# Part of a 31-tap depthwise convolution moved to ScalarE and GpSimd, and 64x64 matrix products spread over four quadrants of TensorE

## The reference, cut to what matters

```python
def causal_dwconv(x, w, b):
    K, C = w.shape                       # K = 31, C = 1024
    y = lax.conv_general_dilated(
        x, w[:, None, :], window_strides=(1,), padding=[(K - 1, 0)],
        dimension_numbers=("NWC", "WIO", "NWC"), feature_group_count=C)
    return y + b

def conformer_conv(x, norm, w1, b1, dw_w, dw_b, ln_g, ln_b, w2, b2):
    h = rms_norm(x, norm) @ w1 + b1
    h = jax.nn.glu(h, axis=-1)
    h = causal_dwconv(h, dw_w, dw_b)
    h = jax.nn.silu(layer_norm(h, ln_g, ln_b))
    return h @ w2 + b2
```

```python
def rwkv_step(S, inp):
    r_t, w_t, k_t, v_t, kk_t, a_t = inp
    sa = jnp.einsum('dbhij,dbhj->dbhi', S, -kk_t)
    S = (S * w_t[..., None, :] + sa[..., :, None] * (kk_t * a_t)[..., None, :]
         + v_t[..., :, None] * k_t[..., None, :])
    y = jnp.einsum('dbhij,dbhj->dbhi', S, r_t)
    return S, y
```

## Time and profile before

| | before |
|---|---|
| median of three runs | 2742.05 us |
| the profiled execution: device time, span | 2743.26 us, 2742.0 us |
| mean granted TensorE clock | 0.965 |
| busy over the span: PE, DVE, ACT, POOL | 93%, 55%, 36%, 8% |
| conformer tile loop, from the glu of tile 0 to the sum of tile 7 | 814.5 to 969.8 us |
| the four quarters of the mixers | about 1850 to 2265 us |

### The profile page before, as it was taken

One profiled execution on the slowest core, in us unless ns is written; L12 is line 12 of the kernel. 1 busy time (PEld: TensorE's weight loads), 2 busy tenths in 40 slices (PEclk: granted clock), 3 DMA queues, 4 the chain that ended last, 5 costly groups with the idle time before them and its releaser, 6 DMA issues. The chain is left out here.

```text
span 2742.0 us, 42005 instructions
## 1 busy us (share of the span) xinstructions
PE 2560.1 (93%) x17980; PEld 1960.5 (72%) x17980; DVE 1499.9 (55%) x1996; ACT 1000.1 (36%) x1467; POOL 220.8 (8%) x190
## 2 busy tenths in 40 slices
PE   8989999999999999999999999997888787979997
PEld 6767878888878877778888878776677675733332
DVE  6776455454559875455454565735675746431112
ACT  4454333232346653243232343325353433321111
POOL 1002010000010000010000110001101100123331
PEclk9999999999999999999999999997998898989998
DMA  4223223222221122222222235322111133389994
GB/s 172 83 73 129 95 77 106 95 92 95 106 93 47 62 92 85 74 104 94 98 101 92 92 142 181 133 92 70 23 31 24 20 79 134 113 351 386 382 380 187
DMA packets 94280, 334.77 MB, mean 122 GB/s; under 512 B 39312, under 2 KB 44688, under 8 KB 60304
## 3 DMA queue, kind: packets, MB, share of 16 engines
q1 hardware_dynamic: 80272, 323.66, 33.1%
q0 software_dynamic: 13824, 8.44, 1.0%
HBM read 368.20 MB, written 30.93 MB: 146 GB/s over the span
## 5 line engine op out<-in xcount | busy, mean ns | idle before, releaser
L557 PE MATMUL bank<-xg_hi,w_hi 128*128 128x512 f32 x1504 | 597.7, 397 | 12.1 <-DVE xg_lo L579 12.1
L557 PE MATMUL bank<-xg_hi,w_lo 128*128 128x512 f32 x1504 | 586.6, 390 | 0.0
L557 PE MATMUL bank<-xg_lo,w_hi 128*128 128x512 f32 x1504 | 586.5, 390 | 0.0
L544 DVE TENSOR_TENSOR w_lo<-w_raw,w_hi 128x2048 fp32r<-128x2048 f32 x165 | 378.7, 2296 | 194.2 <-ACT w_hi L540 194.1
L540 ACT ACTIVATE w_hi<-w_raw 128x2048 fp32r<-128x2048 f32 x165 | 314.3, 1906 | 229.4 <-PE bank L557 206.3
L557 PEld LDWEIGHTS bank<-xg_hi,w_hi 128*128 128x128 f32 x1504 | 282.8, 188 | 77.5 <-DVE w_lo L544 12.0
L557 PEld LDWEIGHTS bank<-xg_lo,w_hi 128*128 128x128 f32 x1504 | 282.9, 188 | 63.8 <-issue 6.0
L557 PEld LDWEIGHTS bank<-xg_hi,w_lo 128*128 128x128 f32 x1504 | 282.6, 188 | 59.2
L557 PE MATMUL bank<-f_h_hi,w_hi 128*128 128x512 f32 x384 | 151.5, 394 | 0.0
L557 PE MATMUL bank<-f_h_hi,w_lo 128*128 128x512 f32 x384 | 150.6, 392 | 0.0
L557 PE MATMUL bank<-f_h_lo,w_hi 128*128 128x512 f32 x384 | 149.2, 389 | 0.0
(11 more groups left out here) (492 smaller groups left out, 4523.8 us busy)
## 6 DMA issues: line engine op xcount, KB each, us to landing
w_raw<-stream SPq DMA_DIRECT2D x165, 1024.0 KB, 4.8
e_over_ring<-expert_rows SPq DMA_DIRECT2D x70, 1024.0 KB, 9.9
e_w_raw<-expert_rows SPq DMA_DIRECT2D x26, 1024.0 KB, 8.3
p_spill<-p_stage SPq DMA_DIRECT2D x36, 256.0 KB, 2.2
na_bias<-bias_na SPq DMA_DIRECT2D x32, 160.0 KB, 4.9
mix_gate<-p_spill SPq DMA_DIRECT2D x16, 256.0 KB, 2.8
e_w_raw<-y_rows SPq DMA_DIRECT2D x8, 512.0 KB, 6.6
rw_rkv<-p_spill SPq DMA_DIRECT2D x12, 256.0 KB, 4.9
```

What stands on the lines that cost most here:

```text
L544: V.tensor_tensor(ring(m)["lo"][m % SLOTS][:, :], ring(m)["raw"][m % RAW][:, :], ring(m)["hi"][m % SLOTS][:, :].bitcast(F32), ALU.subtract ...
L557: return T.matmul(out_ap, lhsT, rhs, start=first, stop=last, skip_group_check=True)
```

## The change

Two things are changed.

1. **Convolution.** TensorE keeps taps 0 to 7 (CONV_C_PE = 8), VectorE keeps taps 18 to 29, ScalarE keeps tap 30. Taps 8 to 17 (CONV_C_POOL = 10) are multiplied by ScalarE: an activation with the tap as scale, the first straight into a sum (c_mu or c_inv, which are free in this stage), nine into three rotating buffers (two halves of `square`, and `root`). GpSimd (`pool_conformer`) adds the nine to the sum, one after the other; a product waits until the addition three before it has been made. VectorE adds the bank and then GpSimd's sum to c_h (`sums(j)`), after tap 22 of the next tile, and for the last tile at the end. ScalarE's diagonals of taps 4 to 7 (in its order) are written in the next turn of the loop.
2. **Mixers.** `products` takes its two banks together and goes over i, then q, then e, so all four quadrants take turns. A product AB, and a new one BL (B times A once more), write the other half ("crossed"), so that X and LT lie in swapped halves; ScalarE copies LT from BL, and VectorE makes XT0 from BA. U reads the half 1-e and writes e. X (read e, write 1-e) and XT (read e, write e) of a level are interleaved. MN goes over four corners, and Z over q within i.

```diff
 LEVELS = 6
-CONV_C_PE = 13
...
+    c_pool = list(range(CONV_C_PE, CONV_C_PE + CONV_C_POOL))[::-1]
+    c_pool_base = CONV_C - 1 - c_pool[0]
+    c_pool_sum = [c_mu, c_inv]
+    c_product = [square[:, 0, :], square[:, 1, :], root[:, :]]
+
+    def c_product_at(j, m):
+        return (j * (CONV_C_POOL - 1) + m - 1) % 3
     c_last_tap = CONV_C - 2
...
+    def pool_conformer(G):
+        for j in range(KT):
+            total = c_pool_sum[j % 2]
+            for m in range(1, CONV_C_POOL):
+                s = CONV_C - 1 - c_pool[m]
+                G.wait_ge(*act_c.at("product", j, m))
+                if m > 1:
+                    G.wait_ge(*pool_c.now())
+                G.tensor_tensor(total[:, s:], total[:, s:], c_product[c_product_at(j, m)][:, s:], ALU.add).then_inc(
+                    *pool_c.mark("tap", j * (CONV_C_POOL - 1) + m - 1))
...
+        def diags(j, first, last):
+            for m in range(first, last):
+                k, n = c_order[m], j * CONV_C_PE + m
+                if n >= 4:
+                    A.wait_ge(*pe_c.at("conv", n - 4))
+                A.activation(c_diag_hi[:, n % 4, :], const("ident"), ACT.Copy, scale=c_tap(j)(k)).then_inc(
+                    *act_c.mark("diag_hi", n))
+                A.wait_ge(*dve_c.at("taps_lo"))
+                A.activation(c_diag_lo[:, n % 4, :], const("ident"), ACT.Copy,
+                             scale=c_taps_lo[:, CONV_C * j + k:CONV_C * j + k + 1]).then_inc(*act_c.mark("diag", n))
+
+        def products(j, first, last):
+            for m in range(first, last):
+                k, at = c_pool[m], c_product_at(j, m)
+                s = CONV_C - 1 - k
+                n = j * (CONV_C_POOL - 1) + m - 1
+                if n >= 3:
+                    A.wait_ge(*pool_c.at("tap", n - 3))
+                A.activation(c_product[at][:, s:], c_t1[:, j % 2, 0:S - s], ACT.Copy, scale=c_tap(j)(k)).then_inc(
+                    *act_c.mark("product", j, m))
+
         for j in range(KT):
...
             A.activation(c_h[:, j, :], c_t1[:, i, :], ACT.Identity, scale=c_tap(j)(CONV_C - 1),
                          bias=vcol("c_dw_b", j)).then_inc(*act_c.mark("last_tap", j))
+            if j:
+                diags(j - 1, 6, CONV_C_PE)
             if j >= 2:
-                A.wait_ge(*pe_c.at("conv", n_diag - len(c_order) - 1))
+                A.wait_ge(*pe_c.at("conv", (j - 1) * CONV_C_PE - 1))
             A.activation(c_t_hi[:, i, C_PAD:], c_t1[:, i, :], ACT.Copy).then_inc(*act_c.mark("t_hi", j))
+            if j >= 2:
+                A.wait_ge(*dve_c.at("h", j - 2))
+            A.activation(c_pool_sum[i][:, c_pool_base:], c_t1[:, i, 0:S - c_pool_base], ACT.Copy,
+                         scale=c_tap(j)(c_pool[0])).then_inc(*act_c.mark("product", j, 0))
+            products(j, 1, 4)
             if j + 1 < KT:
                 act_take(A, place[("pw1", j + 1)])
...
+            for m in range(4):
+                diags(j, m, m + 1)
+                products(j, 4 + m, 5 + m)
+            products(j, 8, CONV_C_POOL)
+        diags(KT - 1, 4, CONV_C_PE)
...
+        def sums(j):
+            V.wait_ge(*pe_c.at("conv", (j + 1) * CONV_C_PE - 1))
+            V.wait_ge(*dve_c.now())
+            V.tensor_tensor(c_h[:, j, c_base:], held("conv", j)[:, c_base:], c_h[:, j, c_base:], ALU.add).then_inc(
+                *dve_c.mark("conv", j))
+            V.wait_ge(*pool_c.at("tap", (j + 1) * (CONV_C_POOL - 1) - 1))
+            V.wait_ge(*dve_c.now())
+            V.tensor_tensor(c_h[:, j, c_pool_base:], c_pool_sum[j % 2][:, c_pool_base:], c_h[:, j, c_pool_base:],
+                            ALU.add).then_inc(*dve_c.mark("h", j))
 
         pointwise(0)
...
-            for k in range(CONV_C_PE, CONV_C - 1):
+            first = CONV_C_PE + CONV_C_POOL
+            for k in range(first, CONV_C - 1):
                 s = CONV_C - 1 - k
                 V.wait_ge(*dve_c.now())
                 stt(V, c_h[:, j, s:], c_t1[:, i, 0:S - s], c_tap(j)(k), c_h[:, j, s:], ALU.mult, ALU.add).then_inc(
                     *dve_c.mark("tap", j, k))
-                if k == CONV_C_PE:
+                if k == first + 4 and j:
+                    sums(j - 1)
+                if k == first + 1:
                     V.wait_ge(*act_c.at("t_hi", j))
                     V.tensor_tensor(c_t_lo[:, i, C_PAD:], c_t1[:, i, :], c_t_hi[:, i, C_PAD:].bitcast(F32),
                                     ALU.subtract).then_inc(*dve_c.mark("t_lo", j))
             if j + 1 < KT:
                 pointwise(j + 1)
-            n_last += len(c_order)
-            V.wait_ge(*pe_c.at("conv", n_last))
-            V.wait_ge(*dve_c.now())
-            V.tensor_tensor(c_h[:, j, c_base:], held("conv", j)[:, c_base:], c_h[:, j, c_base:], ALU.add).then_inc(
-                *dve_c.mark("h", j))
+        sums(KT - 1)
         dve_keys(V, 1, 0, 1)
...
+            def products(name, lhs, rhs, freed_by, freed, cross=0):
+                b = [take_bank(T, (name, t, d, q), freed_by, freed, t, q) for q in range(2)]
+                for i in range(4):
+                    for q in range(2):
                         for e in range(2):
                             rows, c = half_rows(q ^ e), half_rows(2 * i + e)
-                            mm = matmul(T, b[half_rows(e), i * HEAD:(i + 1) * HEAD], lhs[rows, c], rhs[rows, c])
-                    mm.then_inc(*done.mark(name, t, q))
...
+            def block_product(b, n, e, out_half, lhs, rhs):
+                return matmul(T, b[half_rows(out_half), n * HEAD:(n + 1) * HEAD], lhs[half_rows(e), n, :],
+                              rhs[half_rows(e), n, :])
 
             T.wait_ge(*by_dve.at("B", t))
-            products("AB", A_, B, by_dve, "X0")
-            products("BA", B, A_, by_act, "LT")
+            products("AB", A_, B, by_dve, "X0", 1)
+            products("BL", B, A_, by_act, "LT", 1)
+            products("BA", B, A_, by_dve, "XT0")
             yield
...
-                block_products(b, one["LT"], one["X"]).then_inc(*done.mark("U", t, l))
+                for n in range(8):
+                    for e in range(2):
+                        mm = block_product(b, n, 1 - e, e, one["LT"], one["X"])
+                mm.then_inc(*done.mark("U", t, l))
...
                 T.wait_ge(*by_act.at("U", t, l))
                 if l < LEVELS - 1:
-                    b = take_bank(T, ("X", t, d, l), by_dve, "X", t, l)
-                    block_products(b, XT, one["U"]).then_inc(*done.mark("X", t, l))
+                    b_x = take_bank(T, ("X", t, d, l), by_dve, "X", t, l)
                 b = take_bank(T, ("XT", t, d, l), by_dve, "XT", t, l)
-                block_products(b, one["U"], XT).then_inc(*done.mark("XT", t, l))
+                for n in range(8):
+                    for e in range(2):
+                        if l < LEVELS - 1:
+                            mx = block_product(b_x, n, e, 1 - e, XT, one["U"])
+                        mm = block_product(b, n, e, e, one["U"], XT)
+                if l < LEVELS - 1:
+                    mx.then_inc(*done.mark("X", t, l))
+                mm.then_inc(*done.mark("XT", t, l))
                 yield
             T.wait_ge(*by_dve.at("XT", t, LEVELS - 1))
...
+            corners = [(par, e, half_rows(par), half_rows(e)) for par in range(2) for e in range(2)]
+            for i in range(4):
+                o, o2 = slice(i * HEAD, (i + 1) * HEAD), slice((4 + i) * HEAD, (5 + i) * HEAD)
+                for par, e, hc, rows in corners:
+                    matmul(T, b_eo[e][hc, o], UW[rows, par, i, HEAD:P], tokB[rows, i, hc])
+                for par, e, hc, rows in corners:
+                    matmul(T, b_eo[e][hc, o2], tokB[rows, i, hc], UW[rows, par, i, 0:HEAD], True, False)
+                for par, e, hc, rows in corners:
+                    mm = matmul(T, b_eo[e][hc, o2], tokK[rows, i, hc], rw_tokV[rows, i, hc], False, True)
...
-                A.wait_ge(*by_dve.at("XT0", t, q))
-                A.activation(one["LT"][:, fours(q), :], blocks(held("BA", t, d, q), 4), ACT.Copy).then_inc(
+                A.wait_ge(*by_pe.at("BL", t, q))
+                A.activation(one["LT"][:, fours(q), :], blocks(held("BL", t, d, q), 4), ACT.Copy).then_inc(
                     *done.mark("LT", t, q))
```

More of the change, by code:

```diff
@@ L46 @@
 LEVELS = 6
-CONV_C_PE = 13
+CONV_C_PE, CONV_C_POOL = 8, 10
 def _vector_names():
@@ L1516, in pe_conformer @@
                 pe_keys(T, 1, 0, 1)
-            b = take_bank(T, ("conv", j), dve_c, "h", j)
+            b = take_bank(T, ("conv", j), dve_c, "conv", j)
             for m, k in enumerate(c_order):
@@ L1617, in pointwise @@
                 V.wait_ge(*dve_c.at("h", j - 2))
+                V.wait_ge(*act_c.at("product", j - 2, CONV_C_POOL - 1))
             V.wait_ge(*pe_c.at("c2", j))
@@ L2213, in direction @@
             UW, tokB, tokK = one["UW"], one["tokB"], one["tokK"]
-            for par in range(2):
-                hc = slice(par * HEAD, (par + 1) * HEAD)
```

(23 more changed lines are left out.)

29 lines of the change are left out of this document (7 added, 22 removed).

## The result

The changed kernel takes 2764.56 us, the median of four runs (2762.86 to 2771.01), against 2742.28 us for the kernel before, beside it. The ratio is 1.0086 with a 95% interval of 1.0068 to 1.0103: slower by 22.3 us, 0.8%. The forecast was 2755 us, slower, between 2733 and 2778. The time lies in that range, some 9.5 us above the forecast. The direction and the mechanism for the convolution held. For the mixers the rate of the quadrants was taken too cautiously and their share of the chain too generously, for a reason that was in no part of the prediction.

A forecast was written before the change was run, and what follows sets the result against it. The prediction took TensorE to bound the conformer, VectorE close behind, and a chain of TensorE work, DMA, VectorE steps and waits the mixers. From 2743.3 us, +31 (convolution), -18 (mixers) and -1.2 gave 2755 us, range 2733 to 2778.

The forecast's parts named there:

- Nothing in each other's way: 17 us a tile: Convolution: without contention each engine stays near 16.5 us, so a tile could fall from 19.87 to about 17 us.
- The contention: 0.90 an addition, 7.2 a tile: Convolution: GpSimd additions lengthen VectorE's two-SBUF-input taps by 0.90 us each; one of nine hides, 7.2 us a tile remain.
- New waits at nothing: Convolution: new waits between ScalarE, VectorE and GpSimd, and for banks, cost nothing because TensorE has 7 us of room.
- The quadrants: Mixers: products on four quadrants in turn take 18 ns a matmul, between 14.5 and 23, saving 8.7 us a quarter.
- The share of the chain: Mixers: about half of TensorE's saving lies on the chain, so 35 x 0.51 = -18 us, between -9 and -25.
- (1): Convolution rival: ScalarE's products space the additions, so the engines don't hinder each other; 17 us a tile, 2704 us, chance 0.05.
- (2): Rival: only partial contention in the convolution, quadrants give the most; 2733 us, chance 0.12 for faster by over 5 us.
- (3): Rival: convolution loss and mixer gain cancel, +22 - 20, within 5 us of 2743; chance 0.15.
- (4): Mixer rival: quadrants bring nothing, as weights can't be fed faster or DMA or VectorE fills waits; 2771 to 2783, chance 0.10.
- (5): Conformer rival: TensorE, waiting more, loses its clock of 1.00; +90 us at 1.2 GHz, decides under 0.70, chance 0.03.
- The sum: Whole kernel: 2743.3 + 31 for the convolution - 18 for the mixers, less 1.2, gives 2755 us.

The follow-up runs named there:

- e3: The changed kernel with each of GpSimd's 72 additions replaced by a memset, so GpSimd writes SBUF but reads nothing: 2715.95 us, mean of two runs.
- e4: The changed kernel with VectorE's running sum of taps in a PSUM bank, GpSimd still adding in SBUF: 2724.53 us.
- e1: The kernel before with only the convolution part of the change, mixers as before: 2774.32 us, ratio 1.0118.
- e5: The mixer part alone, with quarter 0's MN products repeated many times, two-quadrant order in one direction, four corners in the other: 2799.45 us, one run.
- the mixers alone: The kernel before with only the mixer part of the change, convolution as before: 2729.43 us, ratio 0.9958.

## Why the prediction was right, and where it wasn't

**Nothing in each other's way: 17 us a tile.** Confirmed with a correction: 17.45 us with GpSimd that doesn't read, bound by TensorE, busy for 19.86 of 20. I gave TensorE 16.5 a tile, by taking 15 matmuls at 0.225 off 19.87. The recorded matmuls fell by 12, from 86 to 74 a tile (some records can be missing), and in each tile one tap's matmuls now come 0.4 us late, since its weight load waits for ScalarE's diagonal (PEld for c_diag_lo, 2.7 us in five tiles). The term was 0.9 too small, where it bound nothing in the change.

**The contention: 0.90 an addition, 7.2 a tile.** Right in kind (e3, e4) and in size. Eight additions met taps and the third stood beside the two sums, as I had let one hide: 8 x (1.66 - 0.78) = 7.0 us. The tile became 24.34 where 23.7 was forecast, and the 0.6 is in VectorE's own terms: the glu came 0.24 later, for ScalarE's sigmoid, the first tap waited 1.07 instead of 0.89, and t_lo waited 0.17. One reading was wrong, though the price didn't hang on it: 1.68 for a pair is not "about their sum". The two alone are 0.68 and 1.39, 2.07 together, so the pair is some 0.4 shorter than one after the other. The seven tiles took 984.65 - 815.56 = 169.1 us, +30.0 against the forecast of 26.8 - 1.3. Tile 7 to its last sum took 22.2 us, +6.0 against +4.9, of which +4.6 arrive at ScalarE's reading of the mean. That is +34.6 in the profiled execution; measured by itself the convolution's part cost 32.0 us, forecast 31, within 16 to 43. That the sum is nearer than its terms is in part luck: 26.8 - 1.3 + 4.9 is 30.4, the tiles came out higher, and some 3 us were won back behind the conformer (e1's own trace is 34.4 us behind at the layer norm's reciprocal and 31.9 at the end), for a reason that no run shows.

**New waits at nothing.** Held. TensorE waited for ScalarE's diagonals, and VectorE never for TensorE; ScalarE waited 12 us for GpSimd over the eight tiles, beside 56 that it waited for VectorE; VectorE's wait for ScalarE's last tap went from 0.89 to 1.07 us.

**The quadrants.** I took 18 ns between bounds of 14.5 and 23. It was 14 to 15 at a clock of 1.00, the lower bound, as the rule in the Trainium skill's "TensorEngine Tiling (Array Packing)", section "Tiling Modes", would have it; the traces agree for a level or a product (15.0 and 14 ns) and not for a long stretch (30.3 ns in e5). TensorE's saving was then 12 us in the quarter shown, where I had 8.7.

**The share of the chain: this step failed.** "So 35 x 0.51 = -18 us" assumed that TensorE's time on the chain shrinks in proportion. TensorE was busy for 37 us less in the changed kernel (371 to 334 in the four quarters; 42 less, 329, in the mixers alone), and the part brought 12.9 us, a share of 0.31 to 0.35. Most of the rest became waits for instructions: 3.7 us before, 25.5 in the changed kernel, 27.5 in the mixers alone, so 22 of 24 and 24 of 29 us. In the kernel before, 29 ns a matmul was just what the supply of instructions allows, so nothing of it showed. It can be seen in the trace of before only as a number that I didn't look at. The instruction queue in the quarter from 2057 to 2166, where TensorE ran 1978 matmuls:

```profile
q8 instruction: 15, 0.25, 1.0%
```

That is a 16 KB block for 132 matmuls, and at 14.5 ns a block would last 1.9 us where two blocks start at least 3.3 us apart. The gain that remains is, as I read it, that of short products, which start with instructions at hand after a wait for another engine.

**The rivals.** (1) and (2), no or half contention: refuted by the changed kernel's own taps, and e3 and e4 show what makes them long. (3), both cancel: the parts are +32 and -13. (4), the quadrants bring nothing since the array can't be fed: not so, they brought 12.9 us; but over a long stretch they bring nothing (e5), and the cause is the instructions and not the weights that I named. (5), the clock: it did fall, from 1.00 to between 0.74 and 0.92 in stretches of the conformer loop, but TensorE had the room, as worked out (it would decide below 0.70).

**The sum.** +32.0 and -12.9 where +31 and -18 were forecast: 2755 became 2764.6, and the difference is the mixers' term (5 us), the convolution's (1) and about 3 us by which both together are worse than the two apart, which the spread of the runs (2727 to 2734 for the mixers alone) doesn't let me assign.

## What to carry to other kernels

Before work is given to GpSimd beside VectorE, count VectorE's instructions with two SBUF inputs: each that meets a reading instruction of GpSimd lasts as long as the pair (1.66 us where 0.78 were), unless one of its inputs is moved to PSUM, after which the same division of the convolution won 5 to 9 us instead of losing 32 (the kernel with it and the mixer part won 18). Before small matmuls are packed tighter, divide the distance of two blocks on the profile's instruction queue by the matmuls in a block: a matmul faster than that (here 29 to 30 ns) holds only for bursts. And a saving on an engine's busy time is not yet a saving on the chain; the waits that the profile names "issue" are where to look for the rest.
